# Two transformer blocks on one core: each feed-forward layer as one stage, 1/rms applied behind gate and up, product loops unrolled

## The chip, the cores and the metric

The kernel is written in Bass for one core of a Trainium2 chip. The metric is the device time of one execution in microseconds; profiles are of one execution on that core. Engines are named as in the profile: PE (TensorE matmul), PEld (TensorE weight load), DVE (VectorE), ACT (ScalarE), POOL (GpSimd), SP (SyncE, which issues the DMAs).

## The reference

All data is float32. x is [1, 512, 1024]. A first block of two layers (norm, a product into 3328 columns, two kinds of attention, a product out, norm, add) is followed by a second one. This puts 16 meta tokens ahead (528 tokens) and runs, for each of its two layers, a mixer and a feed-forward layer:

```
def rmsnorm(x, g):
    return x * rsqrt(mean(x * x, axis=-1) + 1e-6) * g

def conv_ffn(h, w_up, w_gate, conv_w, conv_b, w_down):   # h: [528, 1024]
    u = h @ w_up                                          # [528, 2816]
    g = h @ w_gate
    g = causal_conv_over_tokens(g, conv_w, width=3, per channel) + conv_b
    return (silu(g) * u) @ w_down                         # [528, 1024]

h = h + mixer(rmsnorm(h, norm_mix[l]), ...)
h = h + conv_ffn(rmsnorm(h, norm_ffn[l]), ...)
```

The mixer of layer 0 is selected attention beside retention, that of layer 1 stick-breaking attention. A final rmsnorm gives the output [1, 512, 1024].

## The kernel before, in words

The residual stream lies transposed in SBUF as hT [128, 8, 528]: 8 chunks of 128 channels, tokens along the row. The program is a series of stages. Each stage is one nc.Block with a list of instructions per engine; all engines meet at its end. Inside a stage, engines wait for each other on counting semaphores (c.lo_made and so on); a counter's base is moved on after each stage.

**Precision.** A float32 operand of a large product is split into a high part (rounded to the matmul format by a copy on ACT) and a low part (source minus high). A product is three matmuls per chunk: high x high, low activations x high weights, high activations x low weights.

**Weight panels.** Weights come in panels of 2048 (or 1408, 1536) floats per partition. There are two slots. SP loads a panel (L250), ACT makes the high part (L312; for the first panel of a product L257), DVE the low part (L318; first panel L264). PE waits for lo_made, then runs the panel's tiles. A slot's raw panel may be loaded again once its low part is made; its high part may be written again once PE has done the tiles of the panel two back. At a product's end SP loads the first two panels of the next product.

**product_stage** (L267) is used by all products. Its tiles are of two kinds. A T tile (L407) has 128 output channels on the partitions and all tokens in two PSUM banks: for each half of the tokens (264, or 256 in the first block) for each chunk the three matmuls. An N tile (L414) has 128 tokens on the partitions and 256 columns. PE writes tiles into a ring of PSUM tiles; ACT and DVE take them in turn (or DVE alone, solo=True). The panels of a segment are run in pairs by a Fori loop on each engine; the last pair is outside the loop. Stages of four panels run as two pairs with no loop.

**norm_stage** (L559) runs ahead of every product of the second block and computes, for parts=..., the normed activations as high and low parts of rows of 640 floats (TOK padded to PAD). ACT squares each chunk (L585); PE sums squares over partitions with a matmul against ones for each chunk and 128 tokens (L600); ACT takes the root (L589), DVE the reciprocal and five diagonal matrices (L615, L617); PE spreads 1/rms over all partitions (L606). Then per chunk DVE multiplies by gain and spread (L636), ACT makes the high part (L593), and DVE (L623) or POOL (L651) the low part. zero_tails (L662) is a stage of its own ahead of it: POOL clears the padding (L670).

**ffn_layer** (L2074). After zero_tails and norm_stage, a further zero_tails clears two columns ahead of each gate buffer. Then the 2816 inner channels go in two halves of 11 chunks. For each half there are two product stages. The first has 11 panels, each of 128 gate and 128 up columns (two DMAs), with a PSUM ring of 4. ACT copies gate out of PSUM (L2047), DVE convolves in three operations (L2054, L2055, L2057), ACT applies Silu with the bias (L2049), DVE multiplies with up in PSUM (L2061), ACT makes the high part of the result (L2051), and POOL the low part (L2088). The second is the product back, 8 panels of 128 columns with 11 chunks; DVE adds each tile to hT (L1684). Its first panel is split inside the new stage (split_first=False: L257, L264), because a panel's slots and counts are kept per product.

The order of work is written out by hand, as each engine's instruction list; there is no planner.

Of the kernel before, what the change touches and what calls it, by code (L numbers as in the profile page):

```python
# [122 lines left out]
def open_core(nc, ctx, dram):  # L123
# [71 lines left out]
    c.low_made = count("low_made")  # L195
    return c

# [37 lines left out]
class Product:  # L235

    def __init__(self, chunks, cols, segments, dmas=1):
        self.chunks, self.cols, self.segments, self.dmas = chunks, cols, segments, dmas  # L240

# [5 lines left out]
def load_panel(c, sp, product, seg, i, slot):  # L247

    for out, src in seg.load(panel_view(c.raw[slot], product), i):
        sp.dma_start(out, src).then_inc(c.landed[slot].sem, 16)  # L250


def first_panel_hi(c, act, product):

    used = product.chunks * product.cols
    act.wait_ge(c.landed[0].sem, c.landed[0].at(16 * product.dmas))
    act.activation(c.hi[0][:, 0:used], c.raw[0][:, 0:used], ACT.Copy).then_inc(c.hi_made.sem, 1)  # L257


def first_panel_lo(c, dve, product):  # L260

    used = product.chunks * product.cols
    dve.wait_ge(c.hi_made.sem, c.hi_made.at(1))
    dve.tensor_tensor(c.lo[0][:, 0:used], c.raw[0][:, 0:used], c.hi[0][:, 0:used].bitcast(F32),  # L264
                      ALU.subtract).then_inc(c.lo_made.sem, 1)


def product_stage(c, product, acts, split, ring, next_product, solo=False, pool_part=None, split_first=True):
# [4 lines left out]

    nc = c.nc
    segs = product.segments
    used = product.chunks * product.cols
    act_hi, act_lo = acts
    panel_0, tile_0 = [0], [0]
    for s in segs:
        panel_0.append(panel_0[-1] + s.panels)  # L280
        tile_0.append(tile_0[-1] + s.panels * len(s.tiles))
        assert s.panels % 2 == 0 or s is segs[-1]
        assert s.panels == 1 or 2 * len(s.tiles) % ring == 0
    panels, n_tiles = panel_0[-1], tile_0[-1]

    with ExitStack() as stage:
        psum = [c.ps(f"product{r}", [P, 2, 512], stage) for r in range(ring)]

        def pairs_of(eng, body):


            for n, s in enumerate(segs):
                pairs, odd = divmod(s.panels, 2)
                last = n == len(segs) - 1
                peeled = 1 if last and not odd else 0
                if pairs - peeled > 1:
                    with eng.Fori(0, pairs - peeled) as i:
                        body(n, i, 2, False)
                elif pairs - peeled == 1:
                    body(n, 0, 2, False)  # L300
                if peeled:
                    body(n, pairs - 1, 2, True)
                if odd:
                    body(n, pairs, 1, True)

        def make_hi(act, n, p, slot):


            act.wait_ge(c.landed[slot].sem, c.landed[slot].at(product.dmas * 8 * (p - slot + panel_0[n] + 2)))

            act.wait_ge(c.product_ready.sem, c.product_ready.at(tile_0[n] + len(segs[n].tiles) * (p - 1)))
            act.activation(c.hi[slot][:, 0:used], c.raw[slot][:, 0:used], ACT.Copy).then_inc(c.hi_made.sem, 1)  # L312

        def make_lo(dve, n, p, slot):


            dve.wait_ge(c.hi_made.sem, c.hi_made.at(panel_0[n] + p + 1))
            dve.tensor_tensor(c.lo[slot][:, 0:used], c.raw[slot][:, 0:used],  # L318
                              c.hi[slot][:, 0:used].bitcast(F32), ALU.subtract).then_inc(c.lo_made.sem, 1)

        def take_tiles(who, eng, took, n, i, slot):

            s = segs[n]
            for j in range(len(s.tiles)):
                at = slot * len(s.tiles) + j
                if (who == "dve") if solo else (at % 2 == (0 if who == "act" else 1)):

                    eng.wait_ge(c.product_ready.sem,
                                c.product_ready.at(tile_0[n] + 2 * len(s.tiles) * i + at + 1))
                    s.take(who, eng, 2 * i + slot, slot, j, psum[at % ring]).then_inc(took.sem, 1)  # L330

        with nc.Block() as block:
            @block.sync
            def _(sp):

                for n, s in enumerate(segs):
                    def pair(i, count):
                        for slot in range(count):

                            sp.wait_ge(c.lo_made.sem, c.lo_made.at(panel_0[n] + 2 * i + slot - 1))  # L340
                            load_panel(c, sp, product, s, 2 * i + slot, slot)
                    pairs, odd = divmod(s.panels, 2)
                    begin = 1 if n == 0 else 0
                    if pairs - begin > 1:
                        with sp.Fori(begin, pairs) as i:
                            pair(i, 2)
                    elif pairs - begin == 1:
                        pair(begin, 2)
                    if odd:
                        pair(pairs, 1)  # L350
                if next_product is not None:

                    sp.wait_ge(c.lo_made.sem, c.lo_made.at(panels))
                    for slot in range(2):
                        load_panel(c, sp, next_product, next_product.segments[0], slot, slot)

            @block.scalar
            def _(act):
                if not split_first:
                    first_panel_hi(c, act, product)  # L360

                def pair(n, i, count, last):
                    for slot in range(count):

                        if slot == 0 and count == 2:
                            make_hi(act, n, 2 * i + 1, 1)
                        elif not last:
                            make_hi(act, n, 2 * i + 2, 0)
                        take_tiles("act", act, c.act_took, n, i, slot)
                pairs_of(act, pair)  # L370

            @block.vector
            def _(dve):
                if not split_first:
                    first_panel_lo(c, dve, product)

                def pair(n, i, count, last):
                    for slot in range(count):
                        if slot == 0 and count == 2:
                            make_lo(dve, n, 2 * i + 1, 1)  # L380
                        elif not last:
                            make_lo(dve, n, 2 * i + 2, 0)
                        take_tiles("dve", dve, c.dve_took, n, i, slot)
                pairs_of(dve, pair)

            @block.tensor
            def _(pe):
                def pair(n, i, count, last):
                    s = segs[n]
                    for slot in range(count):  # L390

                        pe.wait_ge(c.lo_made.sem, c.lo_made.at(panel_0[n] + 2 * i + slot + 1))
                        w_hi, w_lo = panel_view(c.hi[slot], product), panel_view(c.lo[slot], product)
                        for j, tile in enumerate(s.tiles):
                            at = slot * len(s.tiles) + j
                            out = psum[at % ring]

                            if solo:
                                pe.wait_ge(c.dve_took.sem, c.dve_took.at(tile_0[n] + 2 * len(s.tiles) * i + at - ring + 1))
                            else:  # L400
                                took = c.act_took if at % 2 == 0 else c.dve_took
                                pe.wait_ge(took.sem, took.at(tile_0[n] // 2 + len(s.tiles) * i + (at - ring) // 2 + 1))
                            if tile[0] == "T":
                                for b, (u, v) in enumerate(zip(split[:-1], split[1:])):
                                    for k in range(product.chunks):
                                        for x, (w, a) in enumerate(((w_hi, act_hi), (w_hi, act_lo), (w_lo, act_hi))):
                                            done = pe.matmul(out[:, b, 0:v - u], tile[1](w, k), a[:, k, u:v],  # L407
                                                             start=(k == 0 and x == 0),
                                                             stop=(k == product.chunks - 1 and x == 2))
# [1746 lines left out]
```

## Time and profile before

| | |
|---|---|
| time, median of 3 runs | 3533.53 us (3530.03 to 3536.72) |
| span of the profiled execution | 3526.4 us |
| around the profiled execution's span (median less span) | 7.1 us |
| PE busy | 2846.8 us (81%), 18557 matmuls |
| DVE busy / ACT busy / POOL busy | 1223.9 / 1045.2 / 385.1 us |
| granted TensorE clock, mean | 0.784 |
| DMA | 164.45 MB, 47 GB/s mean |

The span runs from the first to the last instruction of one execution; the median is of runs without the profiler. The profiled execution's own time is its span and what lies around it, for which the page has no number of its own. PE busy is not PE at its peak: at the granted clock of 0.5 (1.2 GHz) the same matmul takes about twice as long as at 1.0 (2.4 GHz). The two feed-forward layers are at 1976 to 2437 us and at 3030 to 3492 us of the span.

### The profile page before, as it was taken

To read this page: it belongs to the slowest core of one execution; us is meant where nothing else is said; L and a number is where in the kernel's file an instruction comes from. 1 tells how busy PE (TensorE), PEld (TensorE's weight loads), DVE (VectorE), ACT (ScalarE), POOL (GpSimd) and SP (SyncE) were. 2 spreads that over 40 slices of the span, in tenths; PEclk is the share of its full clock that TensorE was granted. 3 is DMA by queue.
4 is the path that set the end of the run, shared out by engine and by line. 5 is a ranking of instruction groups with operands and counts; after the bars stand their busy time and mean duration, and the time that the engine had idled before them with its cause. 6 is when DMAs were issued, how large, how long until landed. Compare 5 with 4: busy or idle time off the path is not lost. (4 is left out here: it accounts for less than half of the span.)

```text
span 3526.4 us, 48329 instructions
## 1 busy us (share of the span) xinstructions
PE 2846.8 (81%) x18557; PEld 2634.6 (75%) x18557; DVE 1223.9 (35%) x2105; ACT 1045.2 (30%) x1551; POOL 385.1 (11%) x323
## 2 busy tenths in 40 slices
PE   5983977983978895498399898988986777898988
PEld 4973767972767894497278898988984545898988
DVE  1235233235232323423723243332214444243332
ACT  3233332233332211222132242222225553242222
POOL 0002001002000003201120010010003221010000
PEclk7996566996557996595556799998995667799998
DMA  3310001210000220020001232321210000132321
GB/s 102 96 36 5 1 27 42 90 48 5 1 27 25 72 72 16 24 75 13 29 1 42 60 83 66 96 69 57 96 48 1 0 0 24 48 83 66 96 69 57
DMA packets 232661, 164.45 MB, mean 47 GB/s; under 512 B 7438, under 2 KB 229512, under 8 KB 232420
## 3 DMA queue, kind: packets, MB, share of 16 engines
q1 hardware_dynamic: 232548, 162.91, 15.6%
q8 instruction: 75, 1.23, 0.2%
q14 instruction: 38, 0.31, 0.0%
HBM read 160.76 MB, written 2.14 MB: 46 GB/s over the span
## 5 line engine op out<-in xcount | busy, mean ns | idle before, releaser
L407 PE MATMUL product<-normed_hi,panel_hi 128*128 128x264 f32 (+1 forms) x2128 | 617.2, 290 | 73.8 <-PEq L577 41.0
L407 PE MATMUL product<-normed_lo,panel_hi 128*128 128x264 f32 (+1 forms) x2128 | 615.5, 289 | 0.0
L407 PE MATMUL product<-normed_hi,panel_lo 128*128 128x264 f32 (+1 forms) x2128 | 615.1, 289 | 0.0
L407 PEld LDWEIGHTS product<-normed_hi,panel_hi 128*128 128x128 f32 x2128 | 410.1, 193 | 75.2 <-issue 75.2
L407 PEld LDWEIGHTS product<-normed_hi,panel_lo 128*128 128x128 f32 x2128 | 409.8, 193 | 0.0
L407 PEld LDWEIGHTS product<-normed_lo,panel_hi 128*128 128x128 f32 x2128 | 409.6, 192 | 0.0
L414 PE MATMUL product<-panel_hi,normed_hi 128*128 128x256 f32 (+1 forms) x1336 | 378.3, 283 | 10.4 <-PEq L577 10.4
L318 DVE TENSOR_TENSOR panel_lo<-panel_raw,panel_hi 128x2048 fp32r<-128x2048 f32 (+2 forms) x138 | 293.9, 2130 | 248.0 <-ACT panel_hi L312 248.0
L414 PE MATMUL product<-panel_lo,normed_hi 128*128 128x256 f32 (+1 forms) x1336 | 378.1, 283 | 0.0
L414 PE MATMUL product<-panel_hi,normed_lo 128*128 128x256 f32 (+1 forms) x1336 | 378.1, 283 | 0.0
L312 ACT ACTIVATE panel_hi<-panel_raw 128x2048 fp32r<-128x2048 f32 (+2 forms) x138 | 246.1, 1783 | 442.0 <-PE product L407 381.1
L414 PEld LDWEIGHTS product<-panel_hi,normed_hi 128*128 128x128 f32 x1336 | 257.4, 193 | 10.5 <-issue 10.5
L414 PEld LDWEIGHTS product<-panel_hi,normed_lo 128*128 128x128 f32 x1336 | 257.5, 193 | 0.0
L414 PEld LDWEIGHTS product<-panel_lo,normed_hi 128*128 128x128 f32 x1336 | 257.5, 193 | 0.0
L407 PE MATMUL product<-inner_hi,panel_hi 128*128 128x264 f32 x704 | 206.3, 293 | 36.8 <-DVE panel_lo L264 36.8
L600 PE MATMUL sums<-ones,squares 128*128 128x1 f32 x720 | 149.8, 345 | 72.3 <-ACT squares L585 72.3
L407 PE MATMUL product<-inner_lo,panel_hi 128*128 128x264 f32 x704 | 205.3, 292 | 0.0
L600 PEld LDWEIGHTS sums<-ones,squares 128*128 128x128 f32 x720 | 149.0, 322 | 75.3 <-ACT squares L585 75.3
L407 PE MATMUL product<-inner_hi,panel_lo 128*128 128x264 f32 x704 | 204.9, 291 | 0.0
L407 PE MATMUL product<-y_hi,panel_hi 128*128 128x264 f32 (+1 forms) x576 | 166.2, 289 | 16.9 <-PEq L721 11.1
L938 PE MATMUL scores<-panel_hi 64*128 64x512 f32 (+2 forms) x176 | 96.6, 670 | 92.2 <-POOL panel_lo L897 83.1
L407 PEld LDWEIGHTS product<-inner_hi,panel_hi 128*128 128x128 f32 x704 | 137.6, 195 | 37.6 <-issue 37.6
(258 smaller groups left out, 4989.6 us busy)
## 6 DMA issues: line engine op xcount, KB each, us to landing
panel_raw<-in_w_in_dram SPq DMA_DIRECT2D x26, 1024.0 KB, 5.3
panel_raw<-in_ffn_w_gate_dram SPq DMA_DIRECT2D x44, 512.0 KB, 4.0
panel_raw<-in_ffn_w_up_dram SPq DMA_DIRECT2D x44, 512.0 KB, 5.2
panel_raw<-in_ffn_w_down_dram SPq DMA_DIRECT2D x32, 704.0 KB, 4.9
panel_raw<-in_even_w_in_dram SPq DMA_DIRECT2D x21, 1024.0 KB, 5.2
panel_raw<-in_odd_w_in_dram SPq DMA_DIRECT2D x12, 1024.0 KB, 5.2
panel_raw<-in_w_out_dram SPq DMA_DIRECT2D x8, 1024.0 KB, 5.1
panel_raw<-in_even_w_out_dram SPq DMA_DIRECT2D x8, 768.0 KB, 5.0
```

The lines of the kernel that those rows point to most:

```text
L312: act.activation(c.hi[slot][:, 0:used], c.raw[slot][:, 0:used], ACT.Copy).then_inc(c.hi_made.sem, 1)
L318: dve.tensor_tensor(c.lo[slot][:, 0:used], c.raw[slot][:, 0:used], c.hi[slot][:, 0:used].bitcast(F32), ALU.subtract).then_inc(c.lo_made.se ...
L407: done = pe.matmul(out[:, b, 0:v - u], tile[1](w, k), a[:, k, u:v], start=(k == 0 and x == 0), stop=(k == product.chunks - 1 and x == 2))
L414: done = pe.matmul(out[:, 0, 0:v - u], a[:, k, t * P:(t + 1) * P], w[:, k, u:v], start=(k == 0 and x == 0), stop=(k == product.chunks - 1 ...
L600: done = pe.matmul(sums[:, t:t + 1], squares[k % 2][:, t * P:(t + 1) * P], c.ones[:, 0:1], start=(k == 0 and t == 0), stop=(k == KD - 1), ...
L938: done = pe.matmul(scores[a % s_ring][:, u:v], q[j][rows, b * P:(b + 1) * P], k[j][rows, u:v], start=(w == 0), stop=(w == 2))
```

## The change

There are four edits.

1. **One list of panels.** A Panels object holds every panel of every product of the program in order. Slot, landing count, hi_made, lo_made and product_ready are counted over the whole program, so any stage can load, or split, a panel of the next product. product_stage loads panel g + 2 while it runs panel g.
2. **No loops in the products.** The Fori loops of product_stage are gone; each engine's list is written out in Python.
3. **Order inside a T tile.** wide_tile runs chunks outside, the three parts next, token halves inside: the two halves follow each other in two PSUM banks.
4. **A feed-forward layer is one stage.** The two zero_tails stages, norm_stage and four product stages become one block. The activations are scaled by the gain alone and split (Parts, rows of 528); 1/rms is worked out beside the first tiles (Rstd: squares summed over chunks on POOL, one matmul per 128 tokens, root, diagonal, spread) and is multiplied in by DVE when it takes gate and up out of PSUM. The first tap of the convolution moves from DVE to ACT, the product of Silu and up to POOL. PE waits per chunk in the layer's first tile (Parts) and in the first tile of each product back (low parts of the inner chunks). The PSUM ring is 4 in all of the layer, and its fourth tile holds sums and spread at first.

The diff, cut to its core:

```diff
+class Panels:
+    def load(self, sp, g):
...
+        product, seg, i, _ = self.list[g]
+        if g >= 2:
+            sp.wait_ge(self.c.lo_made.sem, COUNT_START + g - 1)
+        for out, src in seg.load(panel_view(self.c.raw[g % 2], product), i):
+            sp.dma_start(out, src).then_inc(self.c.landed[g % 2].sem, 16)
+    def hi(self, act, g):
...
+        act.wait_ge(c.landed[g % 2].sem, COUNT_START + self.landings[g])
+        if g >= 2:
+            act.wait_ge(c.product_ready.sem, COUNT_START + self.list[g - 2][3])
+        act.activation(c.hi[g % 2][:, 0:used], c.raw[g % 2][:, 0:used], ACT.Copy).then_inc(c.hi_made.sem, 1)
+    def lo(self, dve, g):
...
+        dve.wait_ge(c.hi_made.sem, COUNT_START + g + 1)
+        dve.tensor_tensor(c.lo[g % 2][:, 0:used], c.raw[g % 2][:, 0:used], c.hi[g % 2][:, 0:used].bitcast(F32),
+                          ALU.subtract).then_inc(c.lo_made.sem, 1)
...
+def wide_tile(pe, out, weight, w_hi, w_lo, act_hi, act_lo, chunks, split, before_chunk=None):
+    for k in range(chunks):
+        if before_chunk is not None:
+            before_chunk(k)
+        for x, (w, a) in enumerate(((w_hi, act_hi), (w_hi, act_lo), (w_lo, act_hi))):
+            for b, (u, v) in enumerate(zip(split[:-1], split[1:])):
+                done = pe.matmul(out[:, b, 0:v - u], weight(w, k), a[:, k, u:v], start=(k == 0 and x == 0),
+                                 stop=(k == chunks - 1 and x == 2))
...
 def product_stage(...):
-                pairs_of(act, pair)
+                for g in range(first, first + n_panels):
+                    if g + 1 < first + n_panels:
+                        panels.hi(act, g + 1)
+                    take_tiles("act", act, c.act_took, g)
...
+class Rstd:
+    def act_square(self, act, k):
+        act.wait_ge(c.sum_added.sem, c.sum_added.at(k - 1))
+        act.activation(self.squares[k % 2][:], self.src[:, k, :], ACT.Square).then_inc(c.squared.sem, 1)
+    def pool_add(self, pool, k):
+        pool.wait_ge(c.squared.sem, c.squared.at(k + 1))
+        if k == 0:
+            pool.tensor_copy(total, self.squares[0][:]).then_inc(c.sum_added.sem, 1)
+        else:
+            pool.wait_ge(c.sum_added.sem, c.sum_added.at(k))
+            pool.tensor_tensor(total, total, self.squares[k % 2][:], ALU.add).then_inc(c.sum_added.sem, 1)
...
+class Parts:
+    def act_hi(self, act, k):
+        act.activation(self.hi[:, k, :], self.src[:, k, :], ACT.Copy,
+                       scale=c.gains[:, self.gain, k:k + 1]).then_inc(c.norm_hi.sem, 1)
+    def dve_lo(self, dve, k):
+        dve.wait_ge(c.norm_hi.sem, c.norm_hi.at(k + 1))
+        dve.scalar_tensor_tensor(out=self.lo[:, k, :], in0=self.src[:, k, :], scalar=c.gains[:, self.gain, k:k + 1],
+                                 in1=self.hi[:, k, :].bitcast(F32), op0=ALU.mult, op1=ALU.subtract).then_inc(c.norm_used_dve.sem, 1)
...
+def ffn_layer(c, layer, products):
+            @block.scalar
+                panels.hi(act, first)
+                for k in range(KD):
+                    parts.act_hi(act, k)
+                for k in range(KD):
+                    norm.act_square(act, k)
+                panels.hi(act, first + 1)
+                norm.act_root(act, sums)
+                norm.act_spread(act, sums)
+                for half in range(2):
+                    for i in range(FF_HALF):
+                        if n:
+                            panels.hi(act, g + 1)
+                        if i:
+                            inner_high(act, n - 1)
...
+                        act.activation(conv[n % 2][:], gated[n % 2][:, 0:TOK], ACT.Copy, scale=taps(half, i)[0]).then_inc(c.tap_made.sem, 1)
+                        act.wait_ge(c.gate_convolved.sem, c.gate_convolved.at(n + 1))
+                        act.activation(conv[n % 2][:], conv[n % 2][:], ACT.Silu, bias=taps(half, i)[3]).then_inc(c.gate_silu.sem, 1)
...
+            @block.vector
+                        if i:
+                            take_up(n - 1, g - 1)
+                        if n:
+                            panels.lo(dve, g + 1)
+                        else:
+                            dve.wait_ge(c.rstd_ready.sem, c.rstd_ready.at(1))
...
+                        dve.tensor_tensor(two(gated[n % 2][:, 2:TOK + 2]),
+                                          psum[tile_at(g, 0) % 4][:].rearrange("p (b n) -> p b n", b=2)[:, :, 0:HALF],
+                                          two(norm.spread[:]), ALU.mult).then_inc(c.dve_took.sem, 1)
...
+            @block.gpsimd
+                for k in range(KD):
+                    norm.pool_add(pool, k)
+                for n in range(2 * FF_HALF):
...
+                    pool.tensor_tensor(inner[n % 2][:], conv[n % 2][:], raised[n % 2][:], ALU.mult).then_inc(c.inner_made.sem, 1)
+                    pool.wait_ge(c.inner_hi.sem, c.inner_hi.at(n + 1))
+                    pool.tensor_tensor(lo[:, n % FF_HALF, :], inner[n % 2][:], hi[:, n % FF_HALF, :].bitcast(F32),
+                                       ALU.subtract).then_inc(c.low_made.sem, 1)
...
+            @block.tensor
+                            pe.wait_ge(c.dve_took.sem, c.dve_took.at(t - 3))
+                            if t == 3:
+                                pe.wait_ge(c.rstd_ready.sem, c.rstd_ready.at(1))
...
+                            if t == 1:
+                                norm.pe_sums(pe, sums)
+                            if t == 2:
+                                norm.pe_spread(pe, sums)
```

## Rows read from the trace of the kernel before

**Rows 1.** The page: the instruction queue, then the costliest product groups.

```profile
q8 instruction: 75, 1.23, 0.2%
...
L407 PE MATMUL product<-normed_hi,panel_hi 128*128 128x264 f32 (+1 forms) x2128 | 617.2, 290 | 73.8 <-PEq L577 41.0
...
L414 PE MATMUL product<-panel_hi,normed_hi 128*128 128x256 f32 (+1 forms) x1336 | 378.3, 283 | 10.4 <-PEq L577 10.4
...
L407 PE MATMUL product<-inner_hi,panel_hi 128*128 128x264 f32 x704 | 206.3, 293 | 36.8 <-DVE panel_lo L264 36.8
...
L407 PE MATMUL product<-y_hi,panel_hi 128*128 128x264 f32 (+1 forms) x576 | 166.2, 289 | 16.9 <-PEq L721 11.1
```

**Rows 2.** Waits of PE, 1990 to 2430 us: us in total, times, longest.

```profile
PE product L407 <- DVE panel_lo L264: 23.8, 3, 9.2
```

**Rows 3.** Windows: us; busy us of PE, PEld, DVE, ACT, POOL; clock; DMA.

```profile
1976.40:2437.30 460.90, 420.15 (x3258) 419.13 (x3258) 157.70 (x160) 128.76 (x132) 36.98 (x32) 0.93 0.27 75
3030.30:3491.90 461.60, 420.87 (x3258) 419.85 (x3258) 157.72 (x160) 128.78 (x132) 36.92 (x32) 0.93 0.26 71
```

**Rows 4.** Timeline from gate and up to down: start us, us, what [idle before].

```profile
2150.09 1.30 POOL L2088 TENSOR_TENSOR inner_lo<-inner,inner_hi 128x528 fp32r<-128x528 f32 x1 [9.71 <-ACT inner_hi L2051]
2151.71 1.38 ACT L257 ACTIVATE panel_hi<-panel_raw 128x1408 fp32r<-128x1408 f32 x1 [1.70 <-PEq L332]
...
2153.12 1.63 DVE L264 TENSOR_TENSOR panel_lo<-panel_raw,panel_hi 128x1408 fp32r<-128x1408 f32 x1 [3.79 <-ACT panel_hi L257]
...
2154.88 0.58 PE L407 MATMUL product<-inner_hi,panel_hi 128*128 128x264 f32 x1 [9.20 <-DVE panel_lo L264]
```

**Rows 5.** Timeline of the norm ahead of the first feed-forward layer.

```profile
1980.56 17.23 PE L600 MATMUL sums<-ones,squares 128*128 128x1 f32 x80 [4.17 <-ACT squares L585]
...
1999.58 2.32 PE L606 MATMUL spread<-diagonal,ones 128*128 128x128 f32 x10 [1.80 <-DVE diagonal L617]
...
2003.46 3.04 POOL L651 TENSOR_TENSOR normed_lo<-normed,normed_hi 128x528 fp32r<-128x528 f32 x2 [23.63 <-ACT normed_hi L593]
2004.09 1.24 DVE L623 TENSOR_TENSOR normed_lo<-normed,normed_hi 128x528 fp32r<-128x528 f32 x1
...
2006.71 0.71 DVE L623 TENSOR_TENSOR normed_lo<-normed,normed_hi 128x528 fp32r<-128x528 f32 x1
```

**Rows 6.** Timeline of the layer's first product matmuls.

```profile
2012.88 0.58 PE L407 MATMUL product<-normed_hi,panel_hi 128*128 128x264 f32 x1 [10.98 <-PEq L666]
...
2017.22 0.31 PE L407 MATMUL product<-normed_lo,panel_hi 128*128 128x264 f32 x1
```

**Rows 7.** Windows of L407 alone: us; busy us of PE, PEld; clock; DMA.

```profile
1910.00:1970.00 60.00, 60.00 (x496) 60.00 (x495) 1.00 0.34 95
2240.00:2300.00 60.00, 60.00 (x488) 60.00 (x487) 1.00 0.26 71
2170.00:2220.00 50.00, 50.00 (x411) 50.00 (x410) 1.00 0.36 100
```

**Rows 8.** Groups by line and form, 1976 to 2013 us: busy us, mean ns.

```profile
L636 DVE SCALAR_TENSOR_TENSOR normed<-hT,gains,spread 128x528 f32<-128x528 f32 x8 | 5.7, 757 | 2.4 <-PE spread L606 2.4
...
L593 ACT ACTIVATE normed_hi<-normed 128x528 fp32r<-128x528 f32 x8 | 5.2, 646 | 7.6 <-DVE normed L636 7.5
...
L264 DVE TENSOR_TENSOR panel_lo<-panel_raw,panel_hi 128x2048 fp32r<-128x2048 f32 x1 | 2.3, 2292 | 18.9 <-ACT panel_hi L257 18.9
...
L257 ACT ACTIVATE panel_hi<-panel_raw 128x2048 fp32r<-128x2048 f32 x1 | 1.9, 1894 | 0.0
```

**Rows 9.** Groups by line and form, 2012 to 2440 us.

```profile
L2088 POOL TENSOR_TENSOR inner_lo<-inner,inner_hi 128x528 f32 x20 | 26.7, 1335 | 305.6 <-ACT inner_hi L2051 305.6
...
L2049 ACT ACTIVATE conv<-conv,taps 128x528 f32<-128x528 f32 x22 | 16.3, 739 | 117.1 <-DVE conv L2057 117.0
...
L1684 DVE TENSOR_TENSOR hT<-hT,product 128x528 f32 x12 | 8.5, 704 | 70.8 <-PE product L407 70.8
```

**Rows 10.** DMA queues, 505 to 556 us: packets, MB, share of 16 engines.

```profile
q8 instruction: 3, 0.05, 0.4%
```

More of the change, by code:

```diff
@@ new lines, in row_tile, with product_stage @@
+def row_tile(pe, out, t, u, v, w_hi, w_lo, act_hi, act_lo, chunks):
+    for k in range(chunks):
+        for x, (w, a) in enumerate(((w_hi, act_hi), (w_hi, act_lo), (w_lo, act_hi))):
+            done = pe.matmul(out[:, 0, 0:v - u], a[:, k, t * P:(t + 1) * P], w[:, k, u:v], start=(k == 0 and x == 0),
+                             stop=(k == chunks - 1 and x == 2))
+    return done
+def product_stage(c, product, acts, split, ring, solo=False):
+    nc, panels = c.nc, c.panels
+    act_hi, act_lo = acts
+    first = product.first
+    n_panels = sum(s.panels for s in product.segments)
+    n_tiles = sum(s.panels * len(s.tiles) for s in product.segments)
+    tile_0 = panels.tiles_before(first)
@@ L321, in take_tiles @@
[L321 to L330, printed above, removed]
+        def take_tiles(who, eng, took, g):
+            _, seg, i, _ = panels.list[g]
+            at = panels.tiles_before(g) - tile_0
+            for j in range(len(seg.tiles)):
+                if (who == "dve") if solo else ((at + j) % 2 == (0 if who == "act" else 1)):
+                    eng.wait_ge(c.product_ready.sem, COUNT_START + tile_0 + at + j + 1)
+                    seg.take(who, eng, i, j, psum[(at + j) % ring]).then_inc(took.sem, 1)
@@ L334, in _ @@
             def _(sp):
[L336 to L355, printed above, removed]
+                for g in range(first, first + n_panels):
+                    panels.load(sp, g + 2)
             @block.scalar
             def _(act):
[L359 to L369, printed above, removed]
@@ L370, in _ @@
-                pairs_of(act, pair)
+                for g in range(first, first + n_panels):
+                    if g + 1 < first + n_panels:
+                        panels.hi(act, g + 1)
+                    take_tiles("act", act, c.act_took, g)
             @block.vector
             def _(dve):
[L374 to L383, printed above, removed]
@@ L384, in _ @@
-                pairs_of(dve, pair)
+                for g in range(first, first + n_panels):
+                    if g + 1 < first + n_panels:
+                        panels.lo(dve, g + 1)
+                    take_tiles("dve", dve, c.dve_took, g)
             @block.tensor
             def _(pe):
[L388 to L409, printed above, removed]
-                            else:
-                                _, t, u, v = tile
-                                for k in range(product.chunks):
-                                    for x, (w, a) in enumerate(((w_hi, act_hi), (w_hi, act_lo), (w_lo, act_hi))):
-                                        done = pe.matmul(out[:, 0, 0:v - u], a[:, k, t * P:(t + 1) * P], w[:, k, u:v],
-                                                         start=(k == 0 and x == 0),
-                                                         stop=(k == product.chunks - 1 and x == 2))
-                            done.then_inc(c.product_ready.sem, 1)
@@ L2077, in ffn_layer, with tile_at @@
+def ffn_layer(c, layer, products):
+    nc, panels = c.nc, c.panels
+    split = token_split(False)
+    per_half = FF_HALF + KD
+    first = products[0].first
+    inner_of = [(half, i, first + half * per_half + i) for half in range(2) for i in range(FF_HALF)]
+    tile_0 = panels.tiles_before(first)
+    def tile_at(g, j):
+        return panels.tiles_before(g) - tile_0 + j
     with ExitStack() as stage:
-        parts = normed_parts(c, stage, 6 + layer, products[0][0])
+        norm = Rstd(c, stage, c.hT, TOK)
+        parts = Parts(c, stage, c.hT, TOK, 6 + layer)
@@ L2096, in ffn_layer @@
[L2096 to L2103 removed]
+        psum = [c.ps(f"product{r}", [P, 1024], stage) for r in range(4)]
```

420 lines of the change are left out of this document (265 added, 155 removed).

## The prediction

> **What bounds the kernel now.** I read the page first. The span is 3526.4 us, and its costliest rows are the three-part products of L407 [rows 1]. The question is therefore how closely TensorE (PE) is kept fed there. The wait list of the first feed-forward layer [rows 2] answers it: its largest row is 23.8 us at three places, where PE has the activations but no split weight panel. The windows give each layer whole, from the last matmul of the product ahead to its own last matmul: 460.9 us and 461.6 us [rows 3]. The timeline of one hand-over [rows 4] shows why PE waits 9.20 us: the last chunk's low part ends at 2151.39, only then does a new stage begin, split its first panel (1.38 us on ACT, 1.63 on DVE) and let PE start. In the norm's timeline [rows 5] PE's idle time starts 4.17 us before 1980.56, so the last matmul ended at 1976.39, and the first product matmul comes at 2012.88 [rows 6]: 36.5 us without product work. Inside the products nothing else stops PE. So a layer is 3168 matmuls (2112 into the inner width, 1056 back) plus those stretches, plus climbs of the clock.
>
> **What a matmul costs.** In windows at full clock (1.00, the 2.4 GHz level) the counts include about two matmuls that stick out at the ends [rows 7]: 60 us / 486 = 123.5 ns on the normed parts (rows of 640 columns), 50 / 409 = 122.2 on the inner parts and 60 / 494 = 121.5 on y (both rows of 528). After an idle stretch the pitch is 220 ns: of the first matmuls of the layer, 19 take from 2012.88 to 2017.22 [rows 6], 4.34 us in place of 2.35, an excess of 2.0 us for each restart.
>
> **The change, part by part.**
>
> *Hand-overs.* One stage holds both halves, and the next panel is split while PE is on the one before (ACT 1.89 us plus DVE 2.29 us [rows 8], under 5 us, against 96 matmuls x 0.122 = 11.7 us). The first down tile waits chunk by chunk. Its last chunk comes due 60 matmuls, 7.3 us, after the last up tile. By then: DVE multiply 0.75, POOL multiply 1.34 [rows 9], ACT copy 0.65 [rows 8], POOL subtract behind DVE's panel split (to 3.8) 1.34, in all 5.2 us. So 23.8 us goes, and with it three of four restarts; I cost the hand-overs at nothing, with a margin of 2.1 us. Per panel DVE has 2.29 + 4 x about 0.75 = 5.3 us, ACT 1.89 + 2 x 0.65 + 0.74 = 3.9 and POOL 2 x 1.34 = 2.7 [rows 8, 9]: none reaches 11.7.
>
> *The norm.* Let E be the end of the last matmul ahead. DVE's add into h (0.70 [rows 9]) and a stage change (2151.39 to 2151.71 [rows 4], 0.3) put the start at E + 1.05. ACT splits the panel to 2.95, then makes eight scaled high parts at 0.66 [rows 8] to 8.2. DVE splits the panel to 5.3, then makes the low parts at 0.8 each (757 ns for such an operation [rows 8], and its semaphore). PE begins at E + 6.2. It starts on the low clock: 2.0 us, as before.
>
> The squares now are summed on POOL: one copy and seven adds at 1.34 to 1.39, from E + 8.9. Here DVE's low parts and POOL's adds meet. The trace shows the pair: DVE's subtract of two SBUF operands takes 0.71 us at 2006.71, when POOL has just ended, and 1.24 us at 2004.09, while POOL is in a subtract since 2003.46 [rows 5]. I take them as taking turns: low parts 5, 6 and 7 end at 11.1, 13.2 and 15.3, PE waits 2.0 us within tile 0, and POOL's last add ends at 15.3 + 5 x 1.39 = 22.2. Without turns PE would wait nothing and POOL end at 19.7: 2.3 us less a layer, 4.6 in all. The Trainium skill, SBUF — State Buffer, "Who interferes with whom", says that a VectorE instruction with two SBUF inputs and a GpSimd one that reads SBUF exclude each other for a whole instruction; by that rule, with which the 1.24 us agrees, the sum holds the 4.6, and without it the time would be 4.6 us lower.
>
> PE reaches the sums at about 21.9, waits 0.3 and makes them in 2.15 (10 passes at 17.23 / 80 = 0.215 us [rows 5]). The second panel is split after the last square, at about 24.3: together. Tile 2 runs 5.9 us; the root and the diagonal hide behind it. The spread is 2.3 us [rows 5] and its copy 0.7, for which tile 3 waits: 3.0. Then comes the stage's own new wait: panel 3's high part stands on ACT behind the first chunk's tap and Silu, so multiply 0.75, tap 0.7, two DVE steps 1.6, Silu 0.8, panel high 1.9 and low 2.3 are 8.3 us after the spread, against 5.9 us of tile 3: PE waits 2.4 us. What is queued behind on DVE is the take of the third tile; it has the whole of the next panel's time. Later panels have 5 us to spare.
>
> *Pitch.* The scaled parts have rows of 528, so I take y's 121.5 for the 2112 matmuls.
>
> *Everything else unrolled.* No edge of a loop shows as PE idle: the list's largest row counts only the three hand-overs [rows 2], and the windows inside a loop are full of work [rows 7]. So I cost the loops at nothing on either side. PE, ACT, DVE and SP wait for the same counts in the same order in the other stages. SP's next panels are asked for one split earlier, which nothing waits for.
>
> *Order in a wide tile.* Both token halves of a chunk now follow each other, in two PSUM banks, for 3 x (2128 + 704 + 576) = 10224 matmuls [rows 1]. No row shows this order. Operand layout alone moves the pitch by 2.0 ns (121.5 to 123.5), so I bound it by 2 ns either way, 20 us, and take 0, since nothing in the rows favours a side.
>
> **The sum, per layer.** 2112 x 0.1215 + 1056 x 0.1222 = 385.6. Added: 6.2 + 2.0 (clock) + 2.0 (tile 0) + 2.45 (sums) + 3.0 (spread) + 2.4 = 18.05. That is 403.7, against 460.9 and 461.6: 57.2 and 57.9 off, 115.1 together. The profiled execution spans 3526.4; the median of the runs, 3533.5, lies 7.1 above, which I carry over: **3418.4**.
>
> **The rivals.**
> - *The new order costs pitch.* Up to 2 ns: 3439. Or gains as much: 3398. For: the pitch depends on operands. Against: every matmul still loads its weights, and nothing else changes. 0.10 and 0.05.
> - *The three interruptions at a layer's start are worse.* If PE falls back to the low level at each (2.0 us x 3), and POOL, ACT and the spread are 5 us late together, that is 11 a layer: 3440. For: after the idle 4.17 us of the norm, and after 9.20 at a hand-over, PE is found at the low level [rows 4 to 6]. Against: the three here are 2.5, 3.0 and 2.4 us, and PE works in most of the first two. 0.12.
> - *The hand-over stays.* The margin of 2.1 us is a sum of six steps. If the two into-down waits stay whole (9.2 plus a restart of 2.0) in both layers, 4 x 11.2 = 45 comes back: 3463. 0.04.
> - *Slower: the unrolled code is fetched as it runs.* In the 51 us around a stage of 384 matmuls and 384 weight loads without a loop, three packets of instructions came [rows 10], one for 256 instructions. Unrolled, 14232 product matmuls (10224, and 3 x 1336 = 4008 in row tiles [rows 1]) and their loads are 111 packets. A packet takes 0.2% x 16 x 3526 / 75 = 1.5 us [rows 1]. If PE stood still for each, that is 167 us on PE's own path: 3585. It decides from 1.04 us a packet on. Against: in that unlooped stage PE had no stop. 0.04. The Trainium skill, Runtime: NRT & Kernel Launch, "Instruction fetch mechanics", says that PE holds 2048 instructions and that blocks of 256 are fetched ahead in sequence, mostly hidden. The packet count agrees; by its holding a whole loop body, the loops of before fetch nothing while they turn, which is what speaks against this change, and by its fetching ahead the cost is near nothing.
>
> **How the numbers follow.** 0.65 for the forecast, the rest as given. A measurement of this kernel can tell about 0.2%, 7 us, from no change. Only the fetch case ends above 3533, so faster 0.95, slower 0.04, within 0.2% 0.01. The range takes in the order's 20 us on both sides, rounded for the sum's small terms below, and above also part of the interruptions: 3394 to 3446.
>
> **What would show it.** The wait list of a layer without DVE panel_lo at the hand-overs; a layer of 404 us by windows; first matmul 6.2 us after the last one ahead; one low-clock stretch a layer instead of four; a gap near 2.4 us ahead of the fifth tile; pitch of 121.5 in gate and up. It is wrong if the pitch of the other wide stages moves, if gaps come every 128 matmuls (a packet of code), or if PE waits for POOL's low part in the first down tile.

## The result and the profile after

The changed kernel takes **3413.98 us** (3412.13 to 3415.59, 4 runs) against 3534.27 us before (3530.03 to 3536.72, 4 runs): ratio 0.9671, interval 0.9657 to 0.9685, 120.3 us less. The forecast was 3418.4, in a range of 3394 to 3446.

First the page: span, PE's row, the instruction queue, and one of the new product groups. 1408 is 2 layers x 2 halves x 11 panels x 2 tiles x 8 chunks x 2 token halves, one of the three products.

```profile
span 3411.2 us, 45824 instructions
...
PE 2788.7 (82%) x18417; PEld 2577.8 (76%) x18417; DVE 1237.9 (36%) x2097; ACT 1033.5 (30%) x1535; POOL 499.4 (15%) x369
...
q8 instruction: 134, 2.20, 0.3%
...
L319 PE MATMUL product<-scaled_hi,panel_hi 128*128 128x264 f32 x1408 | 289.9, 287 | 19.6 <-DVE scaled_lo L2097 12.5
```

The windows of the two feed-forward layers, from the last matmul ahead to the layer's own last one (us; busy us of PE, PEld, DVE, ACT, POOL; clock; DMA share; GB/s), answer to [rows 3]:

```profile
1979.20:2381.20 402.00, 392.23 (x3188) 391.49 (x3188) 164.07 (x156) 123.81 (x124) 95.01 (x55) 0.99 0.31 87
2973.70:3378.10 404.40, 394.35 (x3188) 393.38 (x3188) 164.15 (x156) 123.81 (x124) 95.06 (x55) 0.98 0.29 82
```

922.5 us have become 806.4: 116.1 of the 120.3 us lie in the two layers. The mean clock rose from 0.93 to 0.99 and 0.98, since the three restarts behind waits for a panel are gone; in the second layer the clock fell twice more, close behind two of the new pauses (see the last section). POOL, with the sums of squares and the product of Silu and up added to its low parts, went from 37 to 95 us; in the two layers PE waits for it 0.2 us in all.

PE's waits in the first layer (engine, line waited for: us, times, longest), where [rows 2] had 23.8 us for panel_lo:

```profile
PE product L319 <- DVE scaled_lo L2097: 6.2, 1, 6.2
PE product L319 <- DVE panel_lo L252: 2.8, 2, 1.9
PE product L319 <- ACT rstd_spread L2073: 0.8, 1, 0.8
```

9.8 us in all: the start of the layer, the split of the second and third panel, and the spread. Nothing waits at a hand-over. The timeline from gate and up to down shows it, where [rows 4] had 9.20 us (start us, us, engine, line, operation; the last line is the low part of the last chunk):

```profile
2123.23 0.41 PE L319 MATMUL product<-scaled_hi,panel_lo 128*128 128x264 f32 x2
2123.48 0.41 PE L319 MATMUL product<-inner_hi,panel_hi 128*128 128x264 f32 x2
2123.72 0.41 PE L319 MATMUL product<-inner_lo,panel_hi 128*128 128x264 f32 x2
...
2126.61 1.92 POOL L2236 TENSOR_TENSOR inner_lo<-inner,inner_hi 128x528 fp32r<-128x528 f32 x1 [0.75 <-ACT inner_hi L2137]
```

And the timeline of the layer's start, the counterpart of [rows 5, 6]. PE's last matmul ahead ended at 1979.19 = E. L319 are the products, L2039 POOL's adds of squares over the chunks, L2045 the sums of squares on PE, L2097 the low parts of the activations and L252 those of a panel:

```profile
1984.43 8.04 DVE L2097 SCALAR_TENSOR_TENSOR scaled_lo<-hT,gains,scaled_hi 128x528 fp32r<-128x528 f32 x8
...
1985.34 0.78 PE L319 MATMUL product<-scaled_hi,panel_hi 128*128 128x264 f32 x2 [6.15 <-DVE scaled_lo L2097]
...
1988.57 10.96 POOL L2039 TENSOR_TENSOR square_total<-square_total,squares 128x528 f32<-128x528 f32 x7 [0.16 <-POOL square_total L2036]
...
1999.59 1.28 PE L2045 MATMUL product<-ones,square_total 128*128 128x1 f32 x10
...
2001.73 0.52 PE L319 MATMUL product<-scaled_hi,panel_hi 128*128 128x264 f32 x2 [0.87 <-DVE panel_lo L252]
...
2009.67 0.48 PE L319 MATMUL product<-scaled_hi,panel_hi 128*128 128x264 f32 x2 [0.79 <-ACT rstd_spread L2073]
...
2015.31 2.29 DVE L252 TENSOR_TENSOR panel_lo<-panel_raw,panel_hi 128x2048 fp32r<-128x2048 f32 x1 [2.00 <-ACT panel_hi L244]
...
2017.66 0.51 PE L319 MATMUL product<-scaled_hi,panel_hi 128*128 128x264 f32 x2 [1.90 <-DVE panel_lo L252]
```

The steps can be read off one by one: the first matmul comes at E + 6.15; tiles 0 and 1 end at E + 20.3; then come the sums, tile 3 when the spread is copied, and the fifth tile when the third panel is split.

### The profile page after: what moved, and what is told of

Its sections match the earlier page's. It is cut to its first block and busy times, and to the rows that moved or that the text cites. A ratio compares the mean times of both kernels' runs of the same rounds, so it can differ in the third digit from the quotient of the medians.

```text
span 3411.2 us, 45824 instructions
## 1 busy us (share of the span) xinstructions
PE 2788.7 (82%) x18417; PEld 2577.8 (76%) x18417; DVE 1237.9 (36%) x2097; ACT 1033.5 (30%) x1535; POOL 499.4 (15%) x369
## 5 line engine op out<-in xcount | busy, mean ns | idle before, releaser
L252 DVE TENSOR_TENSOR panel_lo<-panel_raw,panel_hi 128x2048 fp32r<-128x2048 f32 (+2 forms) x155 | 335.1, 2162 | 361.6 <-ACT panel_hi L244 361.6
L319 PE MATMUL product<-scaled_hi,panel_hi 128*128 128x264 f32 x1408 | 289.9, 287 | 19.6 <-DVE scaled_lo L2097 12.5
L319 PE MATMUL product<-scaled_lo,panel_hi 128*128 128x264 f32 x1408 | 289.7, 287 | 0.0
L319 PE MATMUL product<-scaled_hi,panel_lo 128*128 128x264 f32 x1408 | 289.5, 287 | 0.0
L319 PEld LDWEIGHTS product<-scaled_hi,panel_hi 128*128 128x128 f32 x1408 | 221.9, 191 | 20.9 <-DVE panel_lo L252 18.8
L319 PEld LDWEIGHTS product<-scaled_lo,panel_hi 128*128 128x128 f32 x1408 | 221.1, 191 | 0.0
L319 PEld LDWEIGHTS product<-scaled_hi,panel_lo 128*128 128x128 f32 x1408 | 220.9, 191 | 0.0
L319 PE MATMUL product<-normed_hi,panel_hi 128*128 128x264 f32 (+1 forms) x720 | 148.8, 288 | 40.2 <-PEq L541 40.2
L933 PE MATMUL mixed<-rows,e_turned 128*128 x768 | 151.3, 369 | 0.0
L319 PE MATMUL product<-normed_lo,panel_hi 128*128 128x264 f32 (+1 forms) x720 | 148.1, 288 | 0.0
L319 PE MATMUL product<-normed_hi,panel_lo 128*128 128x264 f32 (+1 forms) x720 | 147.9, 287 | 0.0
```

Source lines behind the costliest of these rows:

```text
L252: dve.tensor_tensor(c.lo[g % 2][:, 0:used], c.raw[g % 2][:, 0:used], c.hi[g % 2][:, 0:used].bitcast(F32), ALU.subtract).then_inc(c.lo_made ...
L319: done = pe.matmul(out[:, b, 0:v - u], weight(w, k), a[:, k, u:v], start=(k == 0 and x == 0), stop=(k == chunks - 1 and x == 2))
L933: done = pe.matmul(mixed[n % 2][:, 0:d_v], e_turned[n % 2][0:rows, t, :], v_of(i, j, m, t)[0:rows], start=(t == 0), stop=(t == tiles - 1))
```

## The experiments

In the first four, the kernel before ran beside each on the same chip: 3535.95 us, 17 runs. In the last three it was 3528.59 us, 9 runs, on another chip. Ratios are to the kernel before of the same chip. "Pitch" is the time from the start of one matmul to the start of the next.

### The order alone

In the kernel before, wide tiles get the change's order, and nothing else:

```diff
-for b, (u, v) in enumerate(zip(split[:-1], split[1:])):
-    for k in range(product.chunks):
-        for x, (w, a) in enumerate(((w_hi, act_hi), (w_hi, act_lo), (w_lo, act_hi))):
+for k in range(product.chunks):
+    for x, (w, a) in enumerate(((w_hi, act_hi), (w_hi, act_lo), (w_lo, act_hi))):
+        for b, (u, v) in enumerate(zip(split[:-1], split[1:])):
```

> The kernel before with one edit: in a T tile the token halves are the innermost loop. Theory A (the lower pitch of gate and up after the change, 122.3 ns against 123.7, comes from rows of 528 in place of 640): the order does nothing, pitch on the normed parts stays 123.5 to 123.8, time within 3 us of before. Theory B (the order sets it): normed parts of 264 columns fall by 1.1 to 1.8 ns in 5568 matmuls, inner by 0.7 in 2112, y rises by 0.6 to 0.9 in 960, together 8 to 9 us less than before.

Measured: 3521.12 us, 6 runs, ratio 0.9958 (0.9945 to 0.9972). So in the kernel before the order alone gives 15 us by the medians, more than either theory expected, and theory B's signs hold. The two profiled spans, 3526.4 and 3519.0 us, differ by 7.4 only; the profiled execution of before was a fast one (see the section on the prediction). Windows of its product line (us; busy us of PE and PEld with their counts; clock; DMA), the first two in gate and up of the first layer's two halves, the third in the second layer's first half, the last in down:

```profile
2030.00:2090.00 60.00, 60.00 (x495) 60.00 (x495) 1.00 0.31 85
2240.00:2300.00 60.00, 60.00 (x489) 60.00 (x488) 1.00 0.29 80
3100.00:3160.00 60.00, 60.00 (x492) 60.00 (x491) 1.00 0.32 87
2170.00:2220.00 50.00, 50.00 (x414) 50.00 (x413) 1.00 0.34 95
```

In windows of 60 us the kernel before has 487 to 488 matmuls, in 50 us of down 411 [rows 7]. From start to start, at full clock, gate and up went from 123.7 to 123.8 ns to 121.7, 123.4, 122.5 and 121.7 in the four halves, and down from 122.3 to 121.6: 1056 x (2.0 + 0.4 + 1.3 + 2.0) + 2112 x 0.7 = 7.5 us. The two layers together are 911.3 us against 922.5, 11.2 less. The other 3.7 are mostly matmuls at the low clock: 145 in place of 184 (39 x 0.098 = 3.8). Why one stage gets 121.7 and the next 123.4 in the same order stays open.

### The loops alone

```diff
-                if pairs - peeled > 1:
-                    with eng.Fori(0, pairs - peeled) as i:
-                        body(n, i, 2, False)
+                for i in range(pairs - peeled):
+                    body(n, i, 2, False)
```

(and the same in the loads' loop and in POOL's loop over the inner chunks)

> The kernel before with every loop of the product stages (and of POOL's low parts in them) written out, nothing else. Theory A (unrolling is worth nothing): within 3 us of before, more packets of instructions (some 130 in place of 75), no gap inside the products. Theory B (fetching costs): some 60 further packets at up to 1.5 us are up to 90 us more. Theory C (loop edges cost): a few us less.

Measured: 3530.36 us, 12 runs, ratio 0.9987 (0.9978 to 0.9995), so 2 to 8 us less, and no cost. That fits theory C (loop edges cost a few us) a little better than theory A; the profile, of the slowest of the 12 runs, can't tell them apart. Its instruction queue and its two layers:

```profile
q8 instruction: 135, 2.21, 0.3%
...
1984.10:2445.10 461.00, 420.71 (x3258) 419.71 (x3258) 157.68 (x160) 116.66 (x123) 36.97 (x32) 0.93 0.28 76
3039.40:3500.00 460.60, 420.30 (x3258) 419.30 (x3258) 157.67 (x160) 116.66 (x123) 37.05 (x32) 0.93 0.26 72
```

60 more packets of code, and layers of 461.0 and 460.6 us against 460.9 and 461.6. The waits of PE in the first layer are those of the kernel before (23.5 us for the panels against 23.8), so PE stands still for none of the packets; the fetch rival falls.

### The halves outermost again

In the changed kernel the token halves are outermost in a tile, as before; the chunk waits stay in the first half.

```diff
-    for k in range(chunks):
-        if before_chunk is not None:
-            before_chunk(k)
-        for x, (w, a) in enumerate(...):
-            for b, (u, v) in enumerate(zip(split[:-1], split[1:])):
+    for b, (u, v) in enumerate(zip(split[:-1], split[1:])):
+        for k in range(chunks):
+            if before_chunk is not None and b == 0:
+                before_chunk(k)
+            for x, (w, a) in enumerate(...):
```

> The kernel after with the token halves as the outermost loop of a T tile again. Theory A (halves inside are what gives the per-chunk waits their room): the last chunk of the first down tile is due 30 matmuls, 3.7 us, after the last up tile in place of 7.3, its low part comes at about 5.2, so PE waits 1.5 us at four places; in each layer's first tile PE follows DVE's low parts at 1.0 us a chunk, some 3 us more; 12 us more in all, 3426. Rival (the order matters for the pitch alone): no wait for the low part, change by pitch only, within 5 us of the kernel after.

Measured: 3425.69 us, 4 runs (3416.93 to 3429.80), ratio 0.9686 (0.9666 to 0.9706). The changed kernel has 0.9671 (0.9657 to 0.9685): the intervals overlap, so the whole time alone doesn't show a difference; the layers and waits do. The layers take 407.3 and 407.3 us, against 402.0 and 404.4, so 8.2 us more in place of the 12 expected. PE's waits in the first layer, and the last chunk of the first down tile:

```profile
PE product L319 <- DVE scaled_lo L2097: 8.3, 3, 6.2
PE product L319 <- POOL inner_lo L2236: 2.5, 2, 1.3
PE product L319 <- DVE panel_lo L252: 1.9, 1, 1.9
PE product L319 <- ACT rstd_spread L2073: 0.8, 1, 0.8
...
2126.95 0.39 PE L319 MATMUL product<-inner_hi,panel_hi 128*128 128x264 f32 x1 [1.22 <-POOL inner_lo L2236]
```

Here come the two waits that the changed kernel doesn't have: 2.1 us more within tile 0, and 1.2 to 1.3 us at both hand-overs of a layer. With the halves innermost PE has twice the work per chunk, and the last chunk comes due half a tile later. Pitch, in the same layout: gate and up 121.8 ns in all four halves here. In the four profiles with the new order (the changed kernel twice and the last two variants) it is 122.3 in 14 halves of 16 and 121.7 in two. Down is 122.3 against 121.6. So on the scaled parts the order mostly costs 0.5 ns, where on the normed parts it gave 0.3 to 2.0. For the first layer the parts add up: 2.1 in tile 0, 2.8 at the two hand-overs, some 0.9 for nine more matmuls at the low clock, 1.1 less and 0.7 more by pitch are 5.4 us, against 5.3 measured.

### The norm ahead again

The changed feed-forward stage, but behind the old norm stage: products on normed parts, the two DVE multiplies by a row of ones in place of 1/rms.

```diff
-        norm = Rstd(c, stage, c.hT, TOK)
-        parts = Parts(c, stage, c.hT, TOK, 6 + layer)
+        part_hi, part_lo = normed_parts(c, stage, 6 + layer, products[0])
+        one = c.sb("one_row", [P, TOK], into=stage)
```

> The kernel after, but 1/rms is applied by the old norm stage ahead of the layer (with its own clearing stage), and the new stage multiplies by a row of ones in its place; no sums and no spread in the stage. Theory A (the two parts add up): a layer is about 35.3 us to its first matmul, 2.0 for the clock, 2112 x 0.1235 and 1056 x 0.1216, 426.5 us in all, so 3465 us: of the 120 us, 69 are the hand-overs and the pitch, 51 the norm. Rival (the new stage is fed well only because the norm is inside, or the multiply by 1/rms costs time): a layer far from 426.5.

Measured: 3457.13 us, 4 runs, ratio 0.9780 (0.9764 to 0.9797). The windows of its layers and PE's waits in the first (PEq is PE's own sequencer: there PE waits until it has reached the next stage):

```profile
1976.60:2401.50 424.90, 408.78 (x3258) 408.41 (x3258) 165.03 (x160) 123.89 (x123) 91.72 (x55) 0.96 0.29 83
2996.80:3421.90 425.10, 408.94 (x3258) 408.56 (x3258) 165.32 (x160) 123.87 (x123) 91.75 (x55) 0.96 0.28 78
...
PE product L319 <- PEq L541: 10.2, 1, 10.2
PE sums L564 <- ACT squares L549: 4.2, 1, 4.2
PE spread L570 <- DVE diagonal L581: 1.8, 1, 1.8
```

This splits the gain, and a layer is near the 426.5 us of theory A. All but the norm (one stage with waits per chunk, the order, the loops, the work moved to ACT and POOL): 922.5 - 850.0 = 72.5 us. Of these 47.6 are the six waits for panel_lo, and most of the rest the restarts and the pitch (122.5 ns on the normed parts). The norm beside the product: 850.0 - 806.4 = 43.6 us. By the ratios (0.9780 and 0.9671) it is 78 and 39. What the single list of panels and the moved operations do each by themselves was not measured.

### The third panel split ahead of the spread

In the changed kernel the third panel's high part stands behind the first chunk's tap and Silu; here it is made just before the spread is copied, its low part just after the diagonal.

```diff
                 norm.act_root(act, sums)
+                panels.hi(act, first + 2)
                 norm.act_spread(act, sums)
...
                 norm.dve_diagonal(dve, chain)
+                panels.lo(dve, first + 2)
```

> The kernel after with one edit: the layer's third panel is split right after the root (ACT) and the diagonal (DVE), before the spread, not behind the first chunk's Silu. Theory A (the 2.2 us ahead of the fifth tile is that wait, and in the second layer it helps the clock to fall): the gap is gone in both layers, 4.4 us less, and up to 3.4 more if the second layer's two low-clock stretches go; 3408 to 3410. Rival (something else is late next, the fifth tile waits for a PSUM take or the landing): a gap stays.

### The first panel split in the stage ahead as well

```diff
-                    if g + 1 < first + n_panels:
+                    if g + 1 < first + n_panels or solo:
```

(for ACT's and DVE's splits in the product stage; the feed-forward stage no longer splits its first panel)

> As e5, and the layer's first panel is split at the end of the product stage ahead, beside its last tiles, so that the scaled parts start with the stage. Theory A: PE's first matmul comes 2.7 to 3.0 us after the last one ahead in place of 6.15, POOL's sum starts 1.9 us earlier and now holds PE before the sums by about 1 us; 2 to 3 us less a layer than e5; 3403 to 3406. Rival (POOL's chain of eight sets the time of the sums, not the first matmul): the gain is 1.9 us a layer or less, as a wait before the sums.

### The changed kernel once more, beside these two

> The changed kernel once more, with a profile. If pitch is set by the program, each stage repeats its pitch within 0.1 ns (retention's 1440 row tiles 120.0 ns, against 118.7 before the change); if it moves from run to run, that stage differs by 1 ns. The low clock after the sums of the second layer comes again or not by the phase of the clock's control; the time moves by up to 4 us.

Measured: third panel 3410.71 us (5 runs, ratio 0.9663, 0.9650 to 0.9677); both panels **3406.14 us** (5 runs, 0.9654, 0.9641 to 0.9667); the changed kernel 3414.50 (2 runs, 0.9678, 0.9660 to 0.9696). The waits of PE in the first layer, first with the third panel moved, then with both:

```profile
PE product L319 <- DVE scaled_lo L2097: 6.2, 1, 6.2
PE product L319 <- DVE panel_lo L252: 0.9, 1, 0.9
PE product L319 <- ACT rstd_spread L2073: 0.8, 1, 0.8
```

```profile
PE product L319 <- DVE scaled_lo L2097: 2.7, 1, 2.7
PE product L2045 <- POOL square_total L2039: 2.0, 1, 2.0
PE product L319 <- DVE panel_lo L252: 0.9, 1, 0.9
PE product L319 <- ACT rstd_spread L2073: 0.8, 1, 0.8
```

The stall before the fifth tile (1.9 us of waiting, 2.18 from matmul to matmul) is gone in the first, in both layers, and no other wait has grown. In its second layer the clock no longer fell before the fifth tile, but still fell behind the sums. In the second variant the layer starts 3.4 us sooner, but 2.0 us of it come back at once as a wait for POOL's sum, which had been covered: this is the rival of its expectation. The pause at the sums grew to 4.1 us, and in both layers the low clock followed, at once or within 0.5 us of PE's restart. The two layers are 801.1 and 798.1 us (changed kernel: 806.4). The version with both panels has the lowest median of this study, 8.4 us under the changed kernel on the same chip, but with 2 runs of that one the intervals overlap slightly. For the third panel alone (3.8 us) they overlap widely, and the layers and waits are the evidence. Of the changed kernel's second profile: several stages did not repeat their pitch (see the last section), and its ratio, 0.9678, agrees with the 0.9671 of the result.

## Why the prediction was right

The layers came as the sum had them: 402.0 and 404.4 against 403.7 each, 806.4 against 807.4. The span fell by 3526.4 - 3411.2 = 115.2 us, the sum said 115.1. The mechanism was right; that it came out to 0.1 us was luck, since terms that were wrong by up to 2 us a layer cancel. By its steps:

- **Hand-overs at nothing: right**, and only because of the order. The low part of the last chunk ended 5.05 us after the last up tile (forecast 5.2), and PE needed it 7.3 us after. That margin rests on half a tile of work (3.7 us); with the halves outermost PE does wait there, 1.2 to 1.3 us. Inside the loop POOL's subtract, costed at 1.34, took 2.90 while DVE split a panel (below), which raises POOL's work per panel from 2.7 to 4.2 us, still far below 11.7.
- **First matmul at E + 6.2: right** (6.15 and 6.16). The restart had 21 matmuls at the low clock, 21 x 0.098 = 2.06 us against 2.0.
- **2.0 us of waiting in tile 0: wrong, it was 0.35**, and that is what is left after pitch and low clock; the wait list has no wait there. DVE's eight low parts took 8.04 us, between the 10.0 forecast with turns and the 6.4 without, and ended at E + 13.3 (forecast 15.3). PE at the low clock takes 1.3 us a chunk and came to the last one at about E + 13.4, just behind it. With the halves outermost the wait is there. So the 2.3 us a layer that the prediction put on the turns of DVE and POOL were not in the time, though the turns themselves are in the trace.
- **The sums, 2.45: 2.21, and the spread, 3.0: 1.8.** The durations came from rows at the low clock ([rows 5]; from 1999.5 to 2002 us the granted clock was 0.50): ten passes of the sums at 0.215 us and ten of the spread in 2.32. Here the clock was up, and they took 1.28 and 1.19 us. In the sums the difference went into another wait, 0.87 us for the second panel's low part. PE reached the sums at E + 20.33, as POOL ended its last add (E + 20.34; forecast 21.9 and 22.2).

This is the spread between tiles 2 and 3, in the timeline of the changed kernel, for [rows 5]'s 2.32:

```profile
2007.69 1.19 PE L2067 MATMUL product<-diagonal,ones 128*128 128x128 f32 x10
```

- **The stall, 2.4: 2.18** from matmul to matmul. The six durations behind it add up to 8.05 us, not to the 8.3 of the text, so the stall should have been put at 2.15; from the multiply's start (2009.56) to the end of the split (2017.60) they took 8.04. The sums, the spread and the stall were 1.6 us too high together.
- **Pitch 121.5 in gate and up: 122.3 in three of the four halves (121.7 in the second layer's first), 121.8 in the old order.** So y's pitch was close to the right row for the scaled parts, and the order added 0.5 ns. In down it took 0.7 off. In the first layer the sum was 2112 x 0.85 ns = 1.8 us too low in gate and up and 1056 x 0.7 = 0.7 too high in down. The order was bounded by 2 ns either way and taken as 0: right for the sum, since its two signs nearly cancel in these layers; in the kernel before, on normed and inner parts, it is worth 7.5 us.
- **A sign of being wrong did show.** The prediction named a moved pitch of the other wide stages. They moved by 0.6 to 1.8 ns: the first mixer's product from 123.5 to 121.7 ns, the second's from 123.6 to 122.5, and the y products from 121.5 and 121.8 up to 122.4. Some of that is spread between executions (the first mixer's product was at 122.5 ns in the second profile). The falls and rises add up to about 1 us less, so the total hides it.
- **Interruptions: partly the rival.** In the second layer the clock fell twice more, close behind the sums and behind the stall: 32 matmuls at the low clock, 3.1 us. That is most of what sets it 2.4 us above the first, which had six more at its restart. The prediction's sign of one low-clock stretch a layer holds for the first layer only.
- **The mis-sized term was the 7.1 us** taken from the median less the span. In the changed kernel 3412.95 - 3411.2 = 1.75 us lie around the span, and 1.8 to 2.4 in the first four experiments; in the runs of the kernel before beside the experiments it is 1.7 to 3.1. So the profiled execution of before was at about 3528 to 3529.5, some 4 to 5 us faster than the median of its runs, and an execution near the fast end had been compared with a median. With 1.7 to 3.1 in place of 7.1 the forecast would have been 3413 to 3414.4; the error of 4.4 us is this term.

## What to carry to other kernels

Count what stands between the last work of one stage and the first of the next: here three waits of some 8 us in a layer, each with a climb of the clock behind it, were, with a small share for the pitch, over 60% of the gain (72.5 of 116.1 us), and the norm's idle stretch the rest. A wait per chunk is hidden only if the engine has more work per chunk than its suppliers need, so the order inside a tile belongs to that sum. And when the first wait at a stage's start is shortened, look at once for what it had covered: of 3.4 us won there, 2.0 came back as a wait for POOL.

## What the runs showed of the hardware

**DVE and POOL take turns.** The changed kernel's DVE low parts take 8.04 us for eight while POOL adds; with the first panel split earlier DVE is nearly done when POOL's first operation begins, and they take 5.52. POOL's subtract beside a panel split of DVE, from the timeline of the changed kernel:

```profile
2015.88 2.90 POOL L2236 TENSOR_TENSOR inner_lo<-inner,inner_hi 128x528 fp32r<-128x528 f32 x1 [1.00 <-ACT inner_hi L2137]
```

In the kernel before it takes 1.335 on average [rows 9]. It runs from 2015.88, and DVE's split of two SBUF operands lasts from 2015.31 to 2017.60; the 1.2 us after that are about its own time. By the Trainium skill, SBUF — State Buffer, "Who interferes with whom", such a pair excludes each other for a whole instruction; the trace agrees.

**The clock fell or stayed behind nearly the same pause.** The first two windows (columns as above) begin just before PE's restart behind the sums, in the second and in the first layer; the third is the part of the second layer's at the low clock:

```profile
2996.00:3000.60 4.60, 4.37 (x23) 4.37 (x24) 1.35 (x7) 0.00 (x0) 0.00 (x0) 0.63 0.72 201
2001.50:2006.10 4.60, 4.37 (x36) 4.37 (x37) 1.35 (x7) 0.00 (x0) 0.00 (x0) 1.00 0.70 194
2997.20:3000.60 3.40, 3.40 (x18) 3.40 (x17) 0.18 (x1) 0.00 (x0) 0.00 (x0) 0.50 0.98 272
```

The same work is queued, but 23 matmuls run against 36. The pause is counted from the end of the product matmuls to their next start, with the sums in it. Behind one of 2.32 us in the second layer PE ran for 1 us at full pitch, and then the granted clock was 0.50; behind one of 2.21 us in the first layer it stayed at 1.00. In the changed kernel's second profile the pauses were 2.35 us in the second layer and 2.37 in the first, and again only the second layer fell, although its pause was the shorter one. So the length of such a pause doesn't tell what the clock will do, and about 3 us of a layer hang on it. Why it is the second layer each time stays open.

**Pitch changes with order and layout, and from execution to execution.** The retention product's row tiles ran at 120.0 ns in one execution of the changed kernel and at 117.3 in the other, and at 118.7 in the profiles of before and of the six variants: 1440 x 2.7 ns = 3.9 us, as large as the spread of the changed kernel's runs. What sets it is open.
